# A two-block transformer kernel on one core: the modulation's scaling and row sums go from TensorE to GpSimd, and eight of its twelve weight chunks move to later places

## What is computed

```python
mod = (jnp.dot(jax.nn.silu(c), w_ada[l]) + b_ada[l])[:, None, :]
sh1, sc1, g1, sh2, sc2, g2 = jnp.split(mod, 6, axis=-1)
h = rmsnorm(x, norm_mix[l]) * (1.0 + sc1) + sh1
proj = jnp.dot(h, w_in[l])              # retention and differential attention follow
x = x + g1 * jnp.dot(merged, w_out[l])
h2 = rmsnorm(x, norm_ffn[l]) * (1.0 + sc2) + sh2
y = hierarchical_moe(h2, ...)           # 32 experts, two for each token
x = x + g2 * y
return rmsnorm(x, norm_final)
```

## Time and profile before

| | |
|---|---|
| median of 3 runs | 1164.36 us (1164.02 to 1164.74) |
| the profiled execution, its own time | 1165.54 us |
| its span in the trace | 1163.6 us |
| TensorE busy | 1144.1 us of the span |
| VectorE busy | 565.2 us |
| GpSimd busy | 16.1 us |
| mean granted TensorE clock | 0.999 |

### The profile page before, as it was taken

One profiled execution on the slowest core, in us unless ns is written; L12 is line 12 of the kernel. 1 busy time (PEld: TensorE's weight loads), 2 busy tenths in 40 slices (PEclk: granted clock), 3 DMA queues, 4 the chain that ended last, 5 costly groups with the idle time before them and its releaser, 6 DMA issues.

```text
span 1163.6 us, 19322 instructions
## 1 busy us (share of the span) xinstructions
PE 1144.1 (98%) x8093; PEld 879.2 (76%) x8093; DVE 565.2 (49%) x866; ACT 469.9 (40%) x781; POOL 16.1 (1%) x32
## 2 busy tenths in 40 slices
PE   8999999999999999999999999999999999999996
PEld 7988897799988888888888886666666666666654
DVE  5987446687764486486565643222222222222213
ACT  6572133554443364554656433222322333222223
POOL 1300000000000000000000000000000000000000
PEclk9999999999999999999999999999999999999999
DMA  9853968355454646455366469999999999999994
GB/s 317 277 196 125 361 209 321 115 183 179 183 209 164 206 147 187 128 189 160 138 210 251 183 250 420 422 422 422 426 422 422 426 422 422 425 423 423 425 421 182
DMA packets 82701, 332.07 MB, mean 285 GB/s; under 512 B 4555, under 2 KB 6926, under 8 KB 66110
## 3 DMA queue, kind: packets, MB, share of 16 engines
q1 hardware_dynamic: 81236, 328.43, 73.4%
q0 software_dynamic: 1088, 2.34, 1.0%
q10 hardware_dynamic: 298, 0.11, 0.0%
HBM read 329.83 MB, written 1.05 MB: 284 GB/s over the span
## 4 chain that ended last, share of the span: by engine, by line
PE 91%; DMA 6%; DVE 2%; ACT 1%; issue 0%; DVEq 0%; SPq 0%; ACTq 0%
PE bank L1096 17%; PE bank L450 14%; PE bank L452 14%; PE bank L451 14%; PE bank L1115 9%; PE bank L1086 5%; DMA ring<-in_w_exp_down 3%; PE bank L577 3%; DMA ring<-in_w_in 2%; PE bank L443 2%; PE bank L1143 1%; PE bank L1144 1%; PE bank L1103 1%; PE bank L652 0%; PE bank L1129 0%
## 5 line engine op out<-in xcount | busy, mean ns | idle before, releaser
L1828 DVE TENSOR_TENSOR ring_r<-ring,arena_r 128x2048 fp32r<-128x2048 f32 x93 | 212.2, 2291 | 152.2 <-ACT arena_r L1316 150.8
L1316 ACT ACTIVATE arena_r<-ring 128x2048 fp32r<-128x2048 f32 x93 | 177.4, 1917 | 187.8 <-PE bank L452 180.1
L452 PE MATMUL bank<-arena_r,actT_r 128*128 128x512 f32 x384 | 150.4, 392 | 0.0
L450 PE MATMUL bank<-arena_r,tok_r 128*128 128x512 f32 x352 | 140.8, 400 | 0.0
L451 PE MATMUL bank<-ring_r,tok_r 128*128 128x512 f32 x352 | 138.2, 393 | 0.0
L2443 DVE TENSOR_TENSOR arena<-bank,arena 64x512 f32<-64x512 f32 x62 | 42.7, 688 | 175.8 <-PE bank L1115 175.1
L1287 ACT ACTIVATE arena<-bank 128x512 f32<-128x512 f32 (+6 forms) x133 | 57.5, 460 | 115.6 <-PE bank L1103 50.6
L450 PE MATMUL bank<-tok_r,arena_r 128*128 128x256 f32 x352 | 99.3, 282 | 2.3 <-DVE actT_r L1845 1.7
L452 PE MATMUL bank<-tok_r,ring_r 128*128 128x256 f32 x352 | 98.3, 279 | 0.0
L451 PE MATMUL bank<-actT_r,arena_r 128*128 128x256 f32 x352 | 98.2, 279 | 0.0
L450 PE MATMUL bank<-arena_r,arena_r 128*128 128x512 f32 x224 | 89.8, 401 | 0.6 <-DVE ring_r L1828 0.6
(11 more groups left out here) (423 smaller groups left out, 1677.1 us busy)
## 6 DMA issues: line engine op xcount, KB each, us to landing
ring<-in_w_in SPq DMA_DIRECT2D x22, 2048.0 KB, 9.4
ring<-in_w_exp_down SPq DMA_DIRECT2D x22, 2048.0 KB, 21.9
ring<-in_w_exp_gate SPq DMA_DIRECT2D x21, 2048.0 KB, 22.5
arena<-in_w_exp_up SPq DMA_DIRECT2D x21, 2048.0 KB, 24.1
ring<-in_w_ff SPq DMA_DIRECT2D x16, 2048.0 KB, 8.8
ring<-in_w_ada SPq DMA_DIRECT2D x12, 2048.0 KB, 8.8
arena<-in_w_exp_gate SPq DMA_DIRECT2D x11, 2048.0 KB, 22.1
arena<-in_w_exp_down SPq DMA_DIRECT2D x10, 2048.0 KB, 21.8
```

The costliest lines, as they stand in the source:

```text
L450: mm(o, l[0], r[0], start=start, stop=False)
L452: return mm(o, l[1], r[0], start=False, stop=stop)
L1316: A(hi, w, ACT.Copy).then_inc(S["w_high"], 1)
L1828: TT(half(i, ringR)[0], w, hi.bitcast(fp32), ALU.subtract).then_inc(S["w_rest"], 1)
```

## The change

It replaces the `ada` matmuls. GpSimd multiplies each of a chunk's eight row blocks by its column of silu(c) in place (8 `tensor_scalar` of 128x512), waits, and adds them in a tree (4, 2 and 1 `tensor_tensor` of 128x512, a wait behind each level). TensorE then only sums over the partitions: 4 matmuls whose stationary operand is 128x128 of the sum and whose moving operand is one column of ones. The result comes out as columns, so `mod_row` and `mod_turn` are gone and `mod_cols` is one small addition for each chunk. Chunk 0 stands ahead of `win` 6 in the ring; chunks 1 to 3 stay in the delta stretch, 4 to 6 stand behind `ff1` 3, 5 and 7 in the ring (and are used behind `ff1` 3, 6 and 7), 7 to 11 behind `win2` 1, 3, 5, 7 and 9. The delta state has two buffers. `o_turn(1)` moves into the second output product, `w_rest` of the first output halves behind the state updates, `sc2` to step 16.

```diff
-        order = ([("win", c) for c in (3, 4, 7, 5, 0, 1, 2, 6)] + [("ada", c) for c in range(12)]
...
+        ADA_FF1 = {3: 4, 6: 5, 7: 6}
+        ADA_STEP = {1: 7, 3: 8, 5: 9, 7: 10, 9: 11}
+        ADA_BEHIND = {("win", 2): (0,), ("win", 6): (1, 2, 3), ("ff1", 3): (4,), ("ff1", 5): (5,), ("ff1", 7): (6,),
+                      ("win2", 1): (7,), ("win2", 3): (8,), ("win2", 5): (9,), ("win2", 7): (10,), ("win2", 9): (11,)}
...
-                    for k in range(KT):
-                        for j in range(4):
-                            i = mm(bk[32 * j:32 * j + 32, 0:P], csb[:, 32 * k:32 * k + 32],
-                                   w[:, k, j * P:(j + 1) * P], start=(k == 0), stop=(k == KT - 1))
...
+            def ada(c):
+                pe.wait_ge(S["pool_step"], POOL_BIAS + 4 * (c + 1))
+                w = weights("ada", c)
+                bk = begin(f"mod{c}")
+                for j in range(4):
+                    i = mm(bk[:, j:j + 1], w[:, 0, j * P:(j + 1) * P], ones[:, 0:1], start=True, stop=True)
+                end(i, f"mod{c}")
...
+            ada(0)
...
                 elif l == 1:
-                    ada(3)
+                    ada(1)
                 elif l == 2:
                     att_turn()
+                elif l == 3:
                     ada(2)
-                elif l == 3:
                     att_scores((0, 1))
-                    ada(1)
                 else:
                     att_scores((2, 3))
-                    ada(1)
...
-            ada(2)
+            ada(3)
...
-                        step(STT(ST[:, hs], ST[:, hs], ecd[:, 8 * (n % 2) + 4 * t + h:8 * (n % 2) + 4 * t + h + 1],
+                        step(STT(new[:, hs], old[:, hs], ecd[:, 8 * (n % 2) + 4 * t + h:8 * (n % 2) + 4 * t + h + 1],
...
-                if n < 3:
-                    ada(1)
...
-            mod_turn(3)
...
-            o_turn(1)
-            out_product(1, 0)
+            out_product(1, 0, lambda: o_turn(1))
...
+            def ada(c):
+                n = place[("ada", c)]
+                pool.wait_ge(w_in[n % NR], 16 * (n // NR + 1))
+                w = weights("ada", c)
+                for k in range(KT):
+                    i = nc.gpsimd.tensor_scalar(w[:, k, :], w[:, k, :], cs[:, k:k + 1], None, ALU.mult)
+                chain(pool, i, "pool_step")
+                for n in (4, 2, 1):
+                    for k in range(n):
+                        i = nc.gpsimd.tensor_tensor(w[:, k, :], w[:, k, :], w[:, k + n, :], ALU.add)
+                    chain(pool, i, "pool_step")
+
+            pool.wait_ge(S["c_silu"], 1)
+            pool.wait_ge(S["dscaled"], 4)
+            for c in range(4):
+                ada(c)
```

More of the change, by code:

```diff
@@ L283, in program @@
                   + [("wdiff", c) for c in range(2)] + [("wout2", c) for c in range(2)])
-        order = ([("win", c) for c in (3, 4, 7, 5, 0, 1, 2, 6)] + [("ada", c) for c in range(12)]
-                 + [("wout", c) for c in range(2)]
-                 + [("ff1", c) for c in range(8)] + [("ff2", c) for c in range(8)]
-                 + steps2)
+        ADA_FF1 = {3: 4, 6: 5, 7: 6}
+        ADA_STEP = {1: 7, 3: 8, 5: 9, 7: 10, 9: 11}
+        dense = ([("win", c) for c in (3, 4, 7, 5, 0, 1, 2, 6)] + [("wout", c) for c in range(2)]
+                 + [("ff1", c) for c in range(8)] + [("ff2", c) for c in range(8)] + steps2)
+        ADA_BEHIND = {("win", 2): (0,), ("win", 6): (1, 2, 3), ("ff1", 3): (4,), ("ff1", 5): (5,), ("ff1", 7): (6,),
+                      ("win2", 1): (7,), ("win2", 3): (8,), ("win2", 5): (9,), ("win2", 7): (10,), ("win2", 9): (11,)}
+        order = []
+        for k in dense:
+            order.append(k)
+            order += [("ada", c) for c in ADA_BEHIND.get(k, ())]
         NW = len(order)
@@ L421, in wait_actT @@
                     wait_read(pe, f"{name}{j}")
[L423 to L440, removed]
-                    for k in range(KT):
-                        for j in range(4):
-                            i = mm(bk[32 * j:32 * j + 32, 0:P], csb[:, 32 * k:32 * k + 32],
-                                   w[:, k, j * P:(j + 1) * P], start=(k == 0), stop=(k == KT - 1))
-                    end(i, f"mod{c}")
-                    last_job[place[("ada", c)]] = f"mod{c}"
-            adas = [0]
+            def ada(c):
[5 more added lines that the diff above has]
+                end(i, f"mod{c}")
+                last_job[place[("ada", c)]] = f"mod{c}"
             def mm3(o, l, r, start, stop):
@@ L702, in _ @@
                 t, r = n // 2, C * (n % 2)
-                if n == 0:
-                    for x in (0, 1):
-                        wait_read(pe, f"kc{x}")
-                        wait_read(pe, f"dT3{x}")
-                else:
+                old = states[(n - 1) % 2]
+                if n:
+                    if n == 1:
+                        for x in (0, 1):
+                            wait_read(pe, f"kc{x}")
+                            wait_read(pe, f"dT3{x}")
                     pe.wait_ge(S["s_new"], n)
@@ L809, in _ @@
                 last_job[place[("ff1", c)]] = n
+                if c in ADA_FF1:
+                    ada(ADA_FF1[c])
             bks = [begin(f"y{j}") for j in range(4)]
@@ L1400, in _ @@
                 A(ET[:, t * 512:(t + 1) * 512], ET[:, t * 512:(t + 1) * 512], ACT.Exp).then_inc(S["et_exp"], 1)
-            mods = [0]
-            def mod_row(n):
-                for _ in range(n):
-                    c = mods[0]
-                    mods[0] += 1
-                    bk = wait_full(act, f"mod{c}")
-                    done(copy(mrow[:, c % 3 * P:(c % 3 + 1) * P], bk[:, 0:P]), f"mod{c}")
             def token_copies(n, dst):
@@ L2117, in _ @@
             o_tokens(1)
-            mod_cols(3)
-            for x in range(4):
-                wait_read(dve, f"mc{x}")
+            for c in range(4):
+                wait_read(dve, f"mod{c}")
             step(STT(sc1, modc[:, 8:16], 1.0, col("nmix", 0, 8), ALU.add, ALU.mult))
-            step(STT(sc2, modc[:, 32:40], 1.0, col("nffn", 0, 8), ALU.add, ALU.mult))
             w_rest(F0 + 2)
@@ L2347, in _ @@
                     dve.wait_ge(S["wr_in"], 32)
+                    for c in (6, 7, 8, 9):
+                        wait_read(dve, f"mod{c}")
+                    step(STT(sc2, modc[:, 32:40], 1.0, col("nffn", 0, 8), ALU.add, ALU.mult))
                     s4 = spread.rearrange("p (c k j) -> p c k j", c=2, k=KT)
@@ L2610, in _ @@
             nc.gpsimd.memset(bias[0:C, :, 256:256 + C], NEG).then_inc(S["bias_masked"], 1)
-            wait_full(pool, "mc3")
+            steps["pool_step"] = POOL_BIAS
+            def ada(c):
[11 more added lines that the diff above has]
+            pool.wait_ge(S["dscaled"], 4)
+            for c in range(4):
+                ada(c)
+            wait_full(pool, "mod3")
             pool.dma_start(wr[:, :, 0:4], g["w_router_group_2"][0].rearrange("(k p) n -> p k n", p=P)).then_inc(S["wr_in"], 16)
@@ L2617, in _ @@
             pool.dma_start(rowsB[:, 0:16], g["const"][:, o + P:o + P + 16]).then_inc(S["fold_in"], 16)
+            for c in range(4, 12):
+                ada(c)
             wait_full(pool, "rout1")
```

69 lines of the change are left out of this document (33 added, 36 removed).

## The result

The kernel after takes 1237.3 us (median of 4 runs, 1234.3 to 1238.2) beside 1164.6 for the kernel before on the same chip: a ratio of 1.0621, 95% interval 1.0602 to 1.0639, 6.2% slower. The forecast was 1174, with a range of 1151 to 1184. The side was right and the size was far off: +73 us where I had +10. The profiled execution has a span of 1236.4 us.

What follows compares the result with a forecast made beforehand. TensorE was taken to bound the kernel up to about 700 us. Without disturbance the terms summed to -10.7 us; exclusion's +20.4 made +9.7, so 1174.1 us at the median, range 1151 to 1184.

Steps and rivals of the forecast that it cites:

- GpSimd's time for a chunk: Eight scalings at 0.52 us, seven additions at 1.04 and 0.3 for waits: 11.8 us a chunk.
- Rival (a): GpSimd and VectorE do not disturb each other: -10.7 us, 1153.7; chance 0.40.
- Exclusion: VectorE instructions with two SBUF operands and GpSimd's reading ones wait for each other: +20.4 us; 0.42 together with Rival (c).
- Rival (c): GpSimd keeps the path over whole runs, so VectorE is late instead: +7 us, 1172; 0.42 together with Exclusion.
- TensorE's terms: 26.0 us leave the delta stretch; one-column sums of 0.9 a chunk come, 3.6 + 2.7 + 4.5, plus 1.2 for waits.
- The state loop: Delta stretch: thinner fill lets waits surface behind `do{n}`, +1.0 us, between 0 and 4.
- `o_turn`: Delta stretch, `o_turn(1)`: TensorE still waits for its third output half, without transposes first: +0.8 us, between 0 and 1.5.
- The second state buffer: State loop: it takes away a wait that was already hidden, 0.
- The queue's term: Step 8's weights load late behind chunk 10's, delaying step 6's rope and multiplications: +2.0 us, between 0 and 4.
- rival (d): Exclusion plus a lower TensorE clock after each of four waits: +12 us, 1186; chance 0.10.

Runs made afterwards that it cites:

- e10: The changed kernel with each chunk's fifteen GpSimd instructions replaced by 45 memsets of 512 columns, which read nothing: 1198.7 us, ratio 1.0282.
- e3: The changed kernel without GpSimd's eight scalings of a chunk, the seven additions kept: 1175.3 us, ratio 1.0083.
- e2: The changed kernel without any of GpSimd's arithmetic; TensorE waits for each chunk's load and sums its first block only: 1164.8 us, ratio 0.9988.
- e11: The kernel before with chunks 6 to 11 scaled and added by VectorE, and one chunk in the state loop: 1174.0 us, ratio 1.0081.
- e9: e2 with head squares and VectorE's eight multiplications ahead of step 8's weights, and chunks 10 and 11 behind steps 9 and 12: 1153.2 us, ratio 0.9909.
- e7: The changed kernel with filling matmuls on TensorE behind GpSimd's additions only, before six of the seven waits: 1228.3 us, ratio 1.0546.
- e12: e11 with the six chunks that stay with TensorE's matmuls moved, three into the state loop: 1157.9 us, ratio 0.9945 to the kernel before.
- e1: A separate kernel, computing none of the reference, that times GpSimd's and VectorE's instructions alone and together; GpSimd's scaling alone took 1563 ns.
- e8: The changed kernel with head squares earlier, two-tensor products for GpSimd's scalings, and chunks asked for later or set further apart: 1204.6 us, ratio 1.0330.

## Why the prediction was off

**The step that failed is GpSimd's time for a chunk.** I took the memset of 512 columns for a scaling and twice that for an addition, 11.8 us in all, with 15.6 as the bound from above. The additions were near (1.26 for 1.04). The scaling is 1.56, three times the row that I leaned on, and a chunk is 22 us alone. The bound from above was none: nothing in the trace said that an arithmetic instruction of GpSimd costs at most two memsets. Rival (a) went with it, in which slower instructions alone leave the sum near -8: 22 us a chunk without any reading is 1198.7 (e10). Without the scalings the time is 62 us less (e3); that is all of them, also the 4.2 us a chunk that I had, so what the mis-sizing cost is less.

**Exclusion** was called rightly, but it did not decide the side, as I had said that it would. Without GpSimd's work the change gains nothing (e2), and with chunks of 22 us that read nothing it is already 34 us slower (e10). That the kernel came out slower, as forecast, is in part luck. VectorE's subtraction is 2.40 on the mean (2.29 alone), its 512-column scaling in `ff1` 0.81, which was 0.43. I had 20.4 us for it with a chunk of 11.8. e3, with 9 to 14, measures 10.5; e10 puts it at 39 or more with 22. So the price was there and grew with the mis-sized term. (e3's 1175.3 lies beside my 1174 by chance: none of the gain and half of the price.) Rival (c), GpSimd keeping the path so that VectorE is late instead, is there too: the 4.6 us wait at L563 in e3, and in the kernel after the eight multiplications before the retention's turn take 9.73 us, which were 3.25. It was not the main way; seven waits for GpSimd were.

**TensorE's terms held.** 26.0 leave and 0.9 for each chunk's sums come: the rows give 0.95 where the clock is full, and the lead at `ff2` 4 is 17.2 for 17.2. The state loop and `o_turn` are within that total; none of its terms was measured apart. The second state buffer, which I had at 0, may be worth more once the fill is gone: e11, with one, waits for `new_state` and e2, with two, does not. It was not tried alone.

**The queue's term was mis-sized.** I had +2.0 for the turn of step 7, 0 to 4. It costs about 10, 11.6 with the chunk itself and its clock. I had found the late load of step 8 but followed it only to the multiplications; behind them came the banks that VectorE's rope still held, one place earlier in the rotation because of chunk 10, and then the clock. Without it (e9) the change less GpSimd is at 1153.2, which is rival (a)'s 1153.7 by chance: my sum had 2.0 for the turn and e9 has nothing.

**The clock**, rival (d), came as well: 9 us at least (e7), where I had 12 for waits half as long. Exclusion, (c) and (d), which I had kept apart, were true together, on a chunk twice as long, and so the time lay beyond all of them. By differences of the medians: e9's 1153.2, the turn 11.6 (e2), a 22 us chunk without reads 33.9 (e10), the engines' sharing 38.6, 1237.3.

## What to carry to other kernels

An operation that no row shows has no bound from above by its neighbours; before work is moved to an engine that has done nothing but memsets, measure the instruction alone, and in both forms (the product with a spread column was a third cheaper than the scaling by a scalar). Price a moved piece on its whole way: the engine's time beside a busy neighbour, the ring slot, the place in the bank rotation and the clock that the wait costs. Look at what fill hides before it is taken out of a thin loop: two chunks fewer in a loop with one state buffer cost 16 us. And the same sums can pay on another engine: e12, with six of the twelve chunks' sums on VectorE, is 0.6% faster than the kernel before. All twelve, or VectorE in GpSimd's places, was not tried.

## What the runs showed of the hardware

GpSimd's scaling by a scalar per partition is slower (1563 ns for 128x512) than its product of two tensors (1038), its addition (1260) and its copy (613, L127). Even GpSimd's memset slows one form of VectorE's: a scaling from one SBUF operand to SBUF, 427 to 988 ns, but not an addition or a subtraction of two SBUF operands (682 in e1, 2291 in e10). The Trainium skill (SBUF — State Buffer, who interferes with whom) lets VectorE's one-input scaling enter a mode that takes the shared pair, through which GpSimd also writes; by that rule a memset disturbs it, and the trace agrees. TensorE's clock fell from full to half without any wait over 1.8 us: in e11's state loop at about 176 us, just behind the first wait of 1.7, and it was at half until about 206 us (products of 0.63 us up to 206.03, of 0.39 from 206.74). In e8's it fell to half, from about 178 to 198 us, with no wait in the loop at all. What the chip goes by there is not shown.
